# A two-block model forward on one core: loads of the beginning and the heads in another order, tokens chosen in halves, expert outputs added onto x, and the norms between the blocks moved into the second projection

## What is computed

```python
def first_block(...):
    mod = silu(c) @ ada_w + ada_b                # 6 rows of 1024: sh1, sc1, g1, sh2, sc2, g2; the same for c_ctx
    px = modulate(rmsnorm(x, norm1_g), sh1, sc1) @ w_in
    ...                                          # both directions of the recurrence, gates, short convolution
    x = x + g1 * (concatenate([a_x, b_x]) @ w_out)
    hx = modulate(rmsnorm(x, norm2_g), sh2, sc2)
    x = x + g2 * expert_choice_ffn(hx, router_w, w_gate, w_up, w_down)
    return rmsnorm(x, final_g)

def expert_choice_ffn(h, router_w, w_gate, w_up, w_down):
    cap = 2 * 1024 // 16                         # 128 tokens for each expert
    aff = softmax(h @ router_w, axis=-1)
    vals, idx = lax.top_k(swapaxes(aff, 1, 2), cap)
    xs = h[idx]
    hid = silu(xs @ w_gate) * (xs @ w_up)
    out = (hid @ w_down) * vals[..., None]
    return zeros.at[idx].add(out)

def second_block(x, ...):
    proj = rmsnorm_2(x, norm_gain) @ w_in        # q_a k_a v_a g_a q_b k_b v_b g_b, 3328 columns
    ...                                          # norms of heads, rope, banded and dilated attention, gates
    return x + mixed @ w_out
```

## Time and profile before

| | before |
|---|---|
| median of 3 runs | 2611.59 us |
| profiled execution | 2614.48 us |
| its span in the profile | 2612.7 us |
| PE, DVE, ACT, POOL busy | 83%, 66%, 48%, 26% |
| mean granted clock of PE | 0.933 |
| transfers | 414.5 MB, mean 159 GB/s |

### The profile page before, as it was taken

One profiled execution on the slowest core, in us unless ns is written; L12 is line 12 of the kernel. 1 busy time (PEld: TensorE's weight loads), 2 busy tenths in 40 slices (PEclk: granted clock), 3 DMA queues, 4 the chain that ended last, 5 costly groups with the idle time before them and its releaser, 6 DMA issues. The chain is left out here.

```text
span 2612.7 us, 50661 instructions
## 1 busy us (share of the span) xinstructions
PE 2172.6 (83%) x21068; PEld 1747.6 (67%) x21068; DVE 1714.1 (66%) x2582; ACT 1247.8 (48%) x2311; POOL 675.0 (26%) x469
## 2 busy tenths in 40 slices
PE   4899996799999878907999999991389999678989
PEld 2677785678888527706878888871277777456767
DVE  3665545888888454295999999975368475455642
ACT  3312221576666534316888888854322232454420
POOL 0000011666666102140322333304335443000000
PEclk9999998899999989958999999995599999899989
DMA  7222233233322374266999999966633431000042
GB/s 251 56 61 71 61 85 83 63 69 72 72 65 53 134 278 138 97 257 211 356 389 389 387 393 390 393 237 224 233 105 93 143 108 49 19 1 1 1 161 97
DMA packets 167311, 414.48 MB, mean 159 GB/s; under 512 B 13726, under 2 KB 57900, under 8 KB 167084
## 3 DMA queue, kind: packets, MB, share of 16 engines
q1 hardware_dynamic: 146572, 347.79, 38.1%
q0 software_dynamic: 11648, 42.47, 6.3%
q10 hardware_dynamic: 8864, 20.99, 2.1%
HBM read 356.15 MB, written 55.05 MB: 157 GB/s over the span
## 5 line engine op out<-in xcount | busy, mean ns | idle before, releaser
L1892 DVE TENSOR_TENSOR exp_w_lo<-exp_w,exp_w_hi 128x2048 fp32r<-128x2048 f32 x186 | 414.4, 2290 | 24.3 <-ACT exp_w_hi L1849 24.2
L1849 ACT ACTIVATE exp_w_hi<-exp_w 128x1024 fp32r<-128x1024 f32 x384 | 377.3, 1052 | 78.2 <-PE bank L1815 52.7
L2218 PE MATMUL bank<-w_hi,h_lo 128*128 128x512 f32 (+1 forms) x448 | 175.6, 392 | 34.1 <-DMA h_lo<-h_tiles 25.7
L2187 POOL TENSOR_TENSOR w_lo<-heads_a,w_hi 128x512 fp32r<-128x512 f32 (+1 forms) x104 | 138.3, 1355 | 185.4 <-ACT w_hi L2233 185.4
L2218 PE MATMUL bank<-w_hi,h_hi 128*128 128x512 f32 (+1 forms) x448 | 171.9, 384 | 0.0
L2218 PE MATMUL bank<-w_lo,h_hi 128*128 128x512 f32 (+1 forms) x448 | 171.8, 384 | 0.0
L1815 PE MATMUL bank<-exp_w_hi,xsT_lo 128*128 128x512 f32 x512 | 161.2, 396 | 6.5 <-DVE xsT_lo L1896 6.5
L1815 PE MATMUL bank<-exp_w_lo,xsT_hi 128*128 128x512 f32 x512 | 159.4, 393 | 0.0
L1815 PE MATMUL bank<-exp_w_hi,xsT_hi 128*128 128x512 f32 x512 | 159.4, 393 | 0.0
L1783 POOL DMA_INDIRECT moe_rows<-exp_out,idxT x16 | 25.2, 1575 | 439.4 <-DVE exp_out L1943 439.4
L1762 POOL DMA_INDIRECT xs<-xn_rows,idxT x16 | 115.9, 7242 | 37.3 <-DVE idxT L1914 28.5
(11 more groups left out here) (352 smaller groups left out, 5655.1 us busy)
## 6 DMA issues: line engine op xcount, KB each, us to landing
exp_w<-in_exp_w_gate_dram SPq DMA_DIRECT2D x64, 1024.0 KB, 10.2
exp_w<-in_exp_w_up_dram SPq DMA_DIRECT2D x64, 1024.0 KB, 10.6
exp_w<-in_exp_w_down_dram SPq DMA_DIRECT2D x64, 1024.0 KB, 7.4
heads_a<-in_w_in_dram SPq DMA_DIRECT2D x96, 256.0 KB, 2.7
ada_w_second<-in_ada_w_dram SPq DMA_DIRECT2D x16, 1024.0 KB, 7.1
chunk<-rkv_scratch SPq DMA_DIRECT2D x80, 192.0 KB, 4.0
w_in_ring<-in_w_in_dram SPq DMA_DIRECT2D x26, 512.0 KB, 4.0
rkv_scratch<-work POOLq DMA_DIRECT2D x16, 640.0 KB, 5.9
```

What stands on the lines that cost most here:

```text
L1849: last = act.activation(wh[:, n % RH, k, :], w[:, n % RING, k, :], ACT.Copy)
L1892: dve.tensor_tensor(wl[:, n % RH, :, :], w[:, n % RING, :, :], wh[:, n % RH, :, :], ALU.subtract).then_inc(lo_ok, 1)
L2187: pool.tensor_tensor(wl[:, q % SR, 0:width(q)], w[:, q % WR, 0:width(q)], wh[:, q % SR, 0:width(q)], ALU.subtract).then_inc(w_lo, 1)
L2218: mm = pe.matmul(g.ps[m % 4][:, 0:cols], lhs[:, t % HT, k, :], rhs[:, q % SR, 0:cols], start=(k == 0 and p == 0), stop=(k == KT - 1 and p ...
```

## The change

It keeps what is computed and touches five places. **Beginning:** ten x buffers instead of a ring of five (the five new ones, `x_more`, share bytes with the buffers of w_in's high and low parts, so their first splits wait until PE has turned the last tile); SP issues all ten x tiles, then three ada blocks, two w_in pieces, and the last ada block; ACT issues none. All modulation products follow the tiles. DVE modulates only the even k, ACT the odd ones.

```diff
             for i in range(NX):
-                if i >= XR:
-                    sp.wait_ge(turned, i - XR + 1)
-                src = ctx_v[i] if i < 2 else x_v[i - 2]
-                sp.dma_start(xin[i % XR], src).then_inc(x_in[i % XR], 16)
-                if i == XR - 1:
+                sp.dma_start(xin[i], ctx_v[i] if i < 2 else x_v[i - 2]).then_inc(x_in[i], 16)
+            for b in range(NB):
+                if b == NB - 1:
                     for n in range(WR):
                         load_w(n)
+                sp.dma_start(ada[:, b, :, :], adaw[:, :, b * 512:(b + 1) * 512]).then_inc(ada_in[b], 16)
             for n in range(WR, NT):
                 load_w(n)
...
+            for b in range(NB):
+                if b == NB - 1:
+                    for n in range(WR):
+                        split_w(act, n)
                 take_part(b)
             act.wait_ge(ready, 1)
             for k in range(KT):
                 for lo, hi, j in COLS:
                     last = act.activation(hTh[:, k, lo:hi], xT[:, k, lo:hi], ACT.Identity, scale=a1[:, k, j:j + 1], bias=g.mod[:, k, j:j + 1])
+                if k % 2:
+                    for lo, hi, j in COLS:
+                        last = act.activation(xT[:, k, lo:hi], xT[:, k, lo:hi], ACT.Identity, scale=a1[:, k, j:j + 1], bias=g.mod[:, k, j:j + 1])
                 last.then_inc(h_hi, 1)
...
             for k in range(KT):
                 dve.wait_ge(h_hi, k + 1)
-                for lo, hi, j in COLS:
-                    last = dve.tensor_scalar(xT[:, k, lo:hi], xT[:, k, lo:hi], a1[:, k, j:j + 1], g.mod[:, k, j:j + 1], ALU.mult, ALU.add)
-                step(last)
+                if k % 2 == 0:
+                    for lo, hi, j in COLS:
+                        last = dve.tensor_scalar(xT[:, k, lo:hi], xT[:, k, lo:hi], a1[:, k, j:j + 1], g.mod[:, k, j:j + 1], ALU.mult, ALU.add)
+                    step(last)
                 dve.tensor_tensor(hTl[:, k, :], xT[:, k, :], hTh[:, k, :], ALU.subtract).then_inc(h_lo, 1)
```

```diff
-            dve.tensor_copy(g.valsT[:, :], g.ps[7][:, 0:NE])
-            dve.tensor_copy(g.idxT[:, :], g.ps[7][:, NE:2 * NE]).then_inc(picked, 1)
+            turned = g.ps[7][:, 0:2 * (SECOND + NE)].rearrange("p (a n) -> p a n", a=2)
+            dve.tensor_copy(halves[:, 1], turned[:, :, SECOND:SECOND + NE]).then_inc(later, 1)
+            step(dve.tensor_copy(halves[:, 0], turned[:, :, 0:NE]))
+            dve.wait_ge(flipped, 1)
+            value, index = g.ps[6][:, 0:NE], g.ps[6][:, NE:2 * NE]
+            dve.tensor_tensor(taken[:, :], halves[:, 0, 0], value, ALU.is_ge)
+            step(dve.scalar_tensor_tensor(offset[:, :], halves[:, 0, 1], -float(T // 2), index, ALU.add, ALU.subtract))
+            dve.tensor_tensor(g.valsT[:, :], halves[:, 0, 0], value, ALU.max)
+            step(dve.tensor_tensor(offset[:, :], offset[:, :], taken[:, :], ALU.mult))
+            step(dve.scalar_tensor_tensor(offset[:, :], index, float(T // 2), offset[:, :], ALU.add, ALU.add))
...
-                        last = dve.tensor_scalar(o[:, e % 2, s], g.ps[6 + q][:, :], g.valsT[:, e:e + 1], None, ALU.mult)
+                        last = dve.scalar_tensor_tensor(o[:, e % 2, s], g.ps[6 + q][:, :], g.valsT[:, e:e + 1], g.g2[:, s], ALU.mult, ALU.mult)
```

```diff
-    WR, SR = 6, 14
+    WR, SR = 4, 14
+    AT = {HT: 2 * HT, HT + 1: 2 * HT + 2, HT + 2: 5 * HT, HT + 3: 5 * HT + 2}
+    LATER = {m: t for t, m in AT.items()}
...
+            def turn_rows(t):
+                pe.wait_ge(scaled, t + 1)
+                if t >= 1:
+                    pe.wait_ge(h_lo, t)
+                v = xn[t % 2].rearrange("p a (k n) -> p a k n", n=P)
+                for k in range(KT):
+                    mm = pe.transpose(g.ps[6 + k // 4][:, (k % 4) * P:(k % 4 + 1) * P], v[:, k // 4, k % 4], g.c("ident"))
+                mm.then_inc(turned, 1)
...
             for m, (n, t) in enumerate(tiles):
                 blk, cols = m // HT, BLOCKS[n][1]
-                if n == 0:
-                    pe.wait_ge(h_in[t % HT], 32 * (t // HT + 1))
+                if m < HT:
+                    pe.wait_ge(h_lo, t + 1)
+                    if t + 1 < HT:
+                        turn_rows(t + 1)
+                elif n == 0:
+                    pe.wait_ge(h_in[t % HT], 32)
                 if m >= 4:
...
         @block.scalar
         def _(act):
@@ -2238,8 +2167,36 @@
                 act.dma_start(g.gates[t][:, (0 if BLOCKS[n][2] == "ga" else 512):(512 if BLOCKS[n][2] == "ga" else D)],
...
@@ -2261,6 +2218,12 @@
                 if m >= 1 and tiles[m - 1] in gate_no:
                     store_gate(gate_no[tiles[m - 1]])
 
+                if m - 2 in LATER:
+                    high(LATER[m - 2])
+                if m in LATER:
+                    root(LATER[m], 0)
+                    root(LATER[m], 1)
...
@@ -2272,9 +2235,31 @@
         def _(dve):
             step = Chain(dve, chain_v)
 
-            for q in range(KT):
-                dve.wait_ge(w_hi, q + 1)
-                dve.tensor_tensor(wl[:, q, :], w[:, q % WR, :], wh[:, q, :], ALU.subtract).then_inc(w_lo, 1)
+            def final_norm(t):
+                dve.wait_ge(rooted, t + 1)
+                step(dve.reciprocal(rs[:, 0, t:t + 1], rs[:, 0, t:t + 1]))
+                dve.scalar_tensor_tensor(x[t % HT], x[t % HT], rs[:, 0, t:t + 1], fg, ALU.mult, ALU.mult).then_inc(ok, 1)
+
+            def second_norm(t):
+                dve.wait_ge(rooted2, t + 1)
+                step(dve.reciprocal(rs[:, 1, t:t + 1], rs[:, 1, t:t + 1]))
+                dve.scalar_tensor_tensor(xn[t % 2], x[t % HT], rs[:, 1, t:t + 1], ng, ALU.mult, ALU.mult).then_inc(scaled, 1)
+
+            def low(t):
+                dve.wait_ge(h_hi, t + 1)
+                for i in range(2):
+                    hi, lo = (h[:, 4 * i:4 * i + 4, :] for h in parts_of(t))
+                    last = dve.tensor_tensor(lo, g.ps[6 + i][:, :].rearrange("p (k t) -> p k t", t=P), hi, ALU.subtract)
+                last.then_inc(h_lo, 1)
+
+            dve.wait_ge(rows_in, 32)
+            for i in range(HT + 2):
+                if i < HT:
+                    final_norm(i)
+                if 1 <= i < HT + 1:
+                    second_norm(i - 1)
+                if i >= 2:
+                    low(i - 2)
             dve.wait_ge(gain_in, 64)
 
             for i in (0, 2):
...
+                if m - 2 in LATER:
+                    low(LATER[m - 2])
+                if m in LATER:
+                    final_norm(LATER[m])
+                    second_norm(LATER[m])
```

More of the change, by code:

```diff
@@ L31 @@
 CAP = 128
+SECOND = 32
 KAPPA = float(np.exp(-0.5))
@@ L197, in phase_project @@
         three = sb(nc, ctx, "x_rows", [P, 3, D])
-        xin = [three[:, 0], three[:, 1], three[:, 2], rest[:, 2], rest[:, 3]]
         ss = sb(nc, ctx, "x_ss", [P, NX])
@@ L201, in phase_project @@
         w = sb(nc, ctx, "w_in_ring", [P, WR, KT, P])
+        with ExitStack() as early:
+            more = sb(nc, early, "x_more", [P, 5, D])
         wh = sb(nc, ctx, "w_in_hi", [P, SR, KT, P], F32R)
         wl = sb(nc, ctx, "w_in_lo", [P, SR, KT, P], F32R)
+        xin = [three[:, i] for i in range(3)] + [rest[:, i] for i in (2, 3)] + [more[:, i] for i in range(5)]
         work = sb(nc, ctx, "work", [P, KT, TA])
@@ L1819, in _ @@
             pe.wait_ge(top, 1)
-            pe.transpose(g.ps[7][:, 0:NE], vals[:, :], g.c("ident")[0:NE, 0:NE])
-            pe.transpose(g.ps[7][:, NE:2 * NE], idxf[:, :], g.c("ident")[0:NE, 0:NE]).then_inc(top_t, 1)
+            rows = SECOND + NE
+            pe.transpose(g.ps[7][:, 0:rows], vals[:, :], g.c("ident")[0:rows, 0:rows])
+            pe.transpose(g.ps[7][:, rows:2 * rows], idxf[:, :], g.c("ident")[0:rows, 0:rows]).then_inc(top_t, 1)
+            pe.wait_ge(later, 1)
+            pe.matmul(g.ps[6][:, 0:2 * NE], g.c("flip"), halves[:, 1].rearrange("p a e -> p (a e)"),
+                      start=True, stop=True).then_inc(flipped, 1)
             turn_xs(0)
@@ L2127, in phase_second_project @@
         gt = A[:, WR * 512:(WR + 2) * 512].rearrange("p (r n) -> p r n", r=2)
+        ng = A[:, (WR + 2) * 512:(WR + 4) * 512].rearrange("p (a n) -> p a n", a=2)
+        free = slice(T // 2, T)
+        x = [g.qaT[:, 0:2, free], g.qaT[:, 2:4, free], g.qbT[:, 0:2, free], g.qbT[:, 2:4, free]]
+        xn = [g.kbT[:, 0:2, free], g.kbT[:, 2:4, free]]
+        fg = g.kaT[:, 0:2, free]
+        ss = sb(nc, ctx, "cb_ss", [P, 2, TT])
+        rs = sb(nc, ctx, "cb_rs", [P, 2, TT])
         rope = B[:, 0:1024].rearrange("p (t q c) -> p t q c", t=TT, q=4)
@@ L2298, in _ @@
                 kind, bank = BLOCKS[n][2], g.ps[m % 4]
+                if m == HT * NB:
+                    for i in range(HT):
+                        dve.wait_ge(x2_out[i], 32)
+                    dve.wait_ge(h_out, 32 * HT)
                 if kind in gain_of:
@@ L2685, in phase_second @@
             g.va = sb(nc, heads, "va", [P, TT, AKV * HD])
+            with ExitStack() as early:
```

(5 more changed lines are left out.)

305 lines of the change are left out of this document (110 added, 195 removed).

## The result

The changed kernel takes 2520.8 us, median of 4 runs (2514.0 to 2536.8), against 2613.4 for the kernel before beside it (2610.5 to 2619.8): ratio 0.965, 95% interval 0.960 to 0.970. Forecast were 2508 and 2490 to 2532. The profiled execution has a span of 2517.6, 95.1 less than before; forecast were 103.5 less.

What follows compares the result with a forecast made beforehand. No engine bounds the whole; at each hole one chain must end before PE can begin. Terms 16.5 + 13 + 23 + 51 = 103.5 off 2614.5 give 2511 profiled, 2508 median, range 2490 to 2532 (eight in ten).

Steps and rivals of the forecast that it cites:

- Beginning, -16.5: Start to first projection: earlier loads let PE start at 56, 16 sooner; with h's split, -16.5 us, bounds -10 and -20.
- Heads, -13: Heads: fourth ada piece ahead of second rkv load saves 7.9 of 9.12, four slots speed loads; -13, bounds -8 and -16.
- Choice, -23: Choice of tokens: 48 rows of 512 replace 16 of 1024, shortening DVE's 16 rounds; -23 us, bounds -19 and -25.
- Combine into projection, -51: Combine and second projection: kva end 76 us earlier, then 24.5 given back; -51 net, bounds -35 and -62.
- The four holes: Second projection: PE idle on DVE's norm behind tiles 9, 11, 21 and 23, about 6, 5, 7 and 2 us.
- the 6.1 for tile 4: Second projection, ga block: PE waits after product 9 for tile 4's chain of norms, roots and transposes, 6.1 us.
- The port: Second projection: POOL's splits could make each of eight early norms wait a whole split, 10 us less gain in all.
- The table loads: Second projection, ga block: four extra ACT table loads cost 1.28 us each; a drain of about 1.38 would take 5.5 more.
- (a): Rival: second projection gives most back, as splits hold DVE and PE runs dry; that part -30, total 2529; chance 0.15.
- (c): Rival: POOL's six weight splits end after the choice's indices, half of the 23 lost; 2520 us; chance 0.03.
- (b): Rival: transfers set beginning and heads, last ada block lands at 55; -12 instead of -29.5, total 2525; chance 0.07.
- (d): Rival: clock falls over the experts' 574 us, mean of 0.80 adds 143, 2651; decides from 0.85, 103 us; chance 0.02.

Runs made afterwards that it cites:

- b1_sum: The changed kernel with PE's adding up of the third modulation block moved ahead of the fourth modulation product; 2512.1 us.
- x_whole: The changed kernel with the choice of tokens over whole rows of 1024 again; 2537.8 us.
- s_store: The changed kernel with POOL's stores of the late tiles' h issued two splits later in the second projection; 2520.9 us.
- t_turn: The changed kernel with the late tiles' transposes, high and low parts one product later and POOL's stores of h two splits later; 2503.4 us.
- h_order: The changed kernel with four ada_w_second buffers but the old load order, fourth piece behind the second rkv load; one run, 2523.4 us.

## Why the prediction was right, step by step

**Sum and sign.** Right: 95.1 of 103.5 came, the time lies in the range. Of the 8.4 that are missing, 5.8 are the beginning and 1.6 the heads; 4.3 too much in the experts and 5.1 lost in stages without an edit nearly cancel.

**Beginning, -16.5, measured -10.7.** The mechanism held (transfers first, then one chain behind the last ada block), four sizes did not. The block was to land at 46; PE's product began at 48.03. "Behind it stands what stood behind the last modulation product: 9.05" is the step that failed: it is 10.64, because the order of PE puts the third sum behind the fourth product and DVE's w_in subtractions behind the third sum; the prediction read the order on PE and did not carry it on to DVE. b1_sum, which undoes this order, has 9.08. Half clock cost 2.4 in this execution for the 1 that was put in. And the split of h in two passes, put at 1 less, gave nothing: from the first product to the stage's end it is 369.6 for 369.4. At full clock the product comes at 58.7; 56 was forecast, 61.1 measured.

**Heads, -13, measured -11.4.** Undone one at a time, the order is worth 7.6 and the ring 1.9; together the stage lost 11.4 against before, since each also does part of the other's work. Forecast were 7.9 for the order and 5 for the rest: the ring was over-sized.

**Choice, -23, measured -24.3** from the first MAX8 to the first product (75.8 to 51.5; by x_whole 23.7 from the block's start). A pass was to lose 0.53 of its 1.22 and lost 0.53. POOL, with no zeroing, ended its six splits at 1126.3 and then waited 5.6 for the indices, as said. The other 3 of the stage are the spread of the loop.

**Combine into projection, -51, measured -50.9.** Product 0 came at S + 24.9 for 25.4, DVE's fourth low part ended at S + 42.8 for 43, and its last kva tile at S + 90.0 for 91 to 92.5: here the mechanism held step by step. From the block's start to product 8 it is 80.3 for 156.9, 76.6 less; 76 was forecast. Given back from there to the end of the last product were 315.1 - 290.6 = 24.5, the forecast's 24.5, and 1.1 behind it; but the 24.5 are put together otherwise. The four holes were to be about 6, 5, 7 and 2 and were 2.0, 3.4, 5.8 and 1.7. Against before, products 10, 12, 22 and 24 came 2.2, 4.4, 4.9 and 2.7 later behind the product ahead of them, 14.2 in all, for 20.6 forecast. The step that failed is the 6.1 for tile 4: its chain was not set against product 9 running beside it, as that of tile 5 was. On the other side half clock at products 8, 12 and 16 made the steps to the next product 4.2 longer, for some 3.9 put in; product 16 came 2.8 later, which was not forecast (DVE's heads steps, some of them beside POOL's splits); product 28 1.7 later, for the h tiles; and products 36 and 37 took 2.0 more. That the sum agrees is luck.

**The port.** The prediction weighed that POOL's splits might hold each early norm. All sixteen norms (L2241, L2246) took 1.28 except one at 1.41. Ten had a split beside them. In eight of these the norm began 0.3 to 0.4 ahead of the split, and it was the split that took longer, 2.0 to 2.1 instead of 1.3; in the other two the split had 0.1 and 0.3 left. So the norms were spared by who came first, and no norm of this run met a split that had just begun. The one long row is the multiplication above, 5.10, with four subtractions of POOL in a row beside it. The Trainium skill (SBUF — State Buffer, Who interferes with whom) says that two SBUF inputs on DVE contend with GpSimd's reads and that whoever issues first holds the shared pair for its whole instruction. The norms agree; the long row does so too and goes further, since DVE ended only 0.6 after the fourth of four. What of it reached PE is open: s_store moved the delay and did not remove it.

**The table loads.** ACT in the ga block, behind the first sigmoid:

```profile
1815.27 0.19 ACT L2174 ACTIVATION_READ_ACCUMULATOR kbT<-qaT 128x1 f32 x1
1815.48 1.28 ACT L2177 ACT_TABLE_LOAD   x1
1816.78 0.30 ACT L2177 ACTIVATE cb_rs<-cb_ss,const 128x1 f32<-128x1 f32 x1
```

The ga block has five loads for one, as forecast. Nothing stands ahead of this load or behind it. The Trainium skill (ScalarE: Activation LUTs, What ACT_TABLE_LOAD costs) adds some 1.38 of drain; here a load between two dependent instructions cost its 1.28 alone.

**The rivals.** (a), the second projection giving 20 more back, did not come, nor (c), whose POOL waited for the indices. (b) was right in kind and small: the last block 2 later, the heads 1.6 short. (d) fell: the experts' loop kept its length, 571.0 for 574.1. (At a mean of 0.85 the prediction's own formula gives 101 us, not 103.)

## What to carry to other kernels

When a chain is taken apart and put between the steps of a later stage, its parts should be asked for as early and read as late as the buffers allow: one product more between norm and transposes was worth 11 to 13 us of the stretch and some 16 of the time here. Moving the copies that feed the next products ahead of the inserted work took one wait away and brought another, with no gain in the time: each such order has to be weighed against what it pushes back. A step that is moved must be followed over all engines whose order hangs on it, here PE's sum and DVE's subtractions behind it. An edit that spreads a delay over other rows of the same chain has not removed it: the rows must be added up before "no change" is read as "no cost". Where a stage without an edit differs by up to 9 us between profiles, edits of 2 to 5 us are read from the stretch between two fixed events, not from the time.

## What was unexpected

The recurrence, the same 12304 multiplications each time, took 448.7 to 457.4. The longest had the lowest granted clock (0.93), but the clock alone doesn't order the others: t_turn took 450.1 at 0.944, h_order 452.1 at 0.960. In the attention it nearly does: 272.8 at 0.972, 274.2 at 0.963, 275.7 at 0.951, 276.8 at 0.941, 277.9 at 0.935. One POOL run of four subtractions held a DVE instruction for 4.4 us, and with POOL's store moved nearly the same delay (5.1 for 5.4) stood in three other rows. And a stretch at the beginning lasts 10.6 us in five executions and 12 to 13.3 in five others with the same code there, depending on whether PE comes back at full or half clock from its wait for the last ada block: full after 0.3 to 2.3, half after 3.0 to 4.1. But b1_sum came back from 3.10 at full clock, so the length of the wait does not decide it alone.
